# Seven modulation groups moved from the attentions into the first feed forward, and the softmax divisors turned in one matmul

## What is computed

```python
s_lat = silu(c);  s_ctx = silu(c_ctx)
for i in range(2):
    ml = split(s_lat @ w_ada[i] + b_ada[i], 6)     # w_ada[i] is 1024 x 6144
    mc = split(s_ctx @ w_ada[i] + b_ada[i], 6)     # the context needs none of layer 1 but shift and scale
    u = rms_norm(h, g_pre_mix[i]) * (1 + ml[1]) + ml[0]
    h = h + ml[2] * rms_norm(mixer(u), g_post_mix[i])
    f = mlp(rms_norm(h, g_pre_ff[i]) * (1 + ml[4]) + ml[3])     # square of relu, width 4096
    h = h + ml[5] * rms_norm(f, g_post_ff[i])
```

## Time and profile before

| | us |
|---|---|
| median of three runs (lowest, highest) | 1934.95 (1932.95, 1937.16) |
| the profiled execution | 1936.78 |
| its span | 1934.9 |

### The profile page before, as it was taken

The page is one execution under the profiler, slowest core; times in us unless marked ns, Lnnn a source line. Parts: engine busy times, 40 slices in busy tenths (PEclk is TensorE's granted clock), DMA queues, the critical chain, the costliest instruction groups (busy, mean ns, idle before and its releaser), DMA issues. The chain is left out here.

```text
span 1934.9 us, 37112 instructions
## 1 busy us (share of the span) xinstructions
PE 1869.8 (97%) x15824; PEld 1559.3 (81%) x15824; DVE 1105.8 (57%) x1835; ACT 861.6 (45%) x1559; POOL 211.9 (11%) x249
## 2 busy tenths in 40 slices
PE   7999999999999999999999999999999999899998
PEld 5768998776899788756898888888887798579986
DVE  6566774566667554476557665444444565546643
ACT  5465653446656542465322335322222254655532
POOL 2101221110122100103122211000000011000000
PEclk9999999999999999999999999999999999899999
DMA  7777665467766541353000042333332234024653
GB/s 267 250 256 224 189 183 175 166 227 263 223 166 195 175 142 55 115 174 110 26 4 4 4 151 65 104 119 98 100 107 88 66 99 139 25 88 133 194 180 124
DMA packets 219354, 264.68 MB, mean 137 GB/s; under 512 B 14214, under 2 KB 153782, under 8 KB 214711
## 3 DMA queue, kind: packets, MB, share of 16 engines
q1 hardware_dynamic: 218603, 261.49, 42.4%
q10 hardware_dynamic: 588, 0.82, 0.1%
HBM read 261.20 MB, written 1.09 MB: 136 GB/s over the span
## 5 line engine op out<-in xcount | busy, mean ns | idle before, releaser
L404 PE MATMUL acc<-rounded,rounded 128*128 128x512 f32 (+1 forms) x2552 | 875.1, 343 | 9.6 <-DVE rounded L684 4.1
L405 PE MATMUL acc<-rounded,rounded 128*128 128x512 f32 (+1 forms) x2552 | 867.0, 340 | 0.0
L406 PE MATMUL acc<-rounded,rounded 128*128 128x512 f32 (+1 forms) x2552 | 866.8, 340 | 0.0
L388 DVE TENSOR_TENSOR rounded<-arena,rounded 128x2048 fp32r<-128x2048 f32 (+1 forms) x194 | 434.3, 2241 | 285.9 <-ACT rounded L377 285.8
L404 PEld LDWEIGHTS acc<-rounded,rounded 128*128 128x128 f32 x2552 | 480.6, 188 | 80.1 <-issue 14.7
L405 PEld LDWEIGHTS acc<-rounded,rounded 128*128 128x128 f32 x2552 | 480.7, 188 | 60.0 <-issue 1.9
L406 PEld LDWEIGHTS acc<-rounded,rounded 128*128 128x128 f32 x2552 | 480.5, 188 | 60.0
L377 ACT ACTIVATE rounded<-arena 128x2048 fp32r<-128x2048 f32 (+1 forms) x194 | 362.9, 1873 | 341.6 <-PE acc L406 296.4
L1624 DVE SCALAR_TENSOR_TENSOR arena<-acc,pcol,arena 128x254 f32<-128x254 f32 (+1 forms) x176 | 76.8, 478 | 52.3 <-ACT arena L1605 50.8
L2200 PE MATMUL sc<-arena 64*64 64x64 f32 x2560 | 94.7, 221 | 8.8 <-DVE arena L2350 7.7
L2764 ACT ACTIVATE arena<-acc 128x512 f32<-128x512 f32 (+1 forms) x64 | 31.4, 490 | 159.6 <-PE acc L406 159.6
(11 more groups left out here) (265 smaller groups left out, 1691.6 us busy)
## 6 DMA issues: line engine op xcount, KB each, us to landing
arena<-in_w_ff SPq DMA_DIRECT2D x64, 1024.0 KB, 5.4
arena<-in_w_ada SPq DMA_DIRECT2D x48, 1024.0 KB, 5.1
arena<-in_w_up SPq DMA_DIRECT2D x88, 512.0 KB, 5.1
arena<-in_w_in SPq DMA_DIRECT2D x24, 1024.0 KB, 5.3
arena<-in_w_down SPq DMA_DIRECT2D x20, 1024.0 KB, 5.0
arena<-in_w_out SPq DMA_DIRECT2D x16, 1024.0 KB, 5.1
arena<-in_w_in_even SPq DMA_DIRECT2D x9, 1024.0 KB, 5.3
arena<-in_w_in_odd SPq DMA_DIRECT2D x8, 1024.0 KB, 5.2
```

The costliest lines, as they stand in the source:

```text
L388: dve.tensor_tensor(r32(w), w, r32(high_slot(c)[:, 0:size(c)]), ALU.subtract).then_inc(split_made, 1)
L404: pe.matmul(ps, ah, bh, start=first, stop=False)
L405: pe.matmul(ps, ah, bl, start=False, stop=False)
L406: return pe.matmul(ps, al, bh, start=False, stop=last)
```

## The change

Four things are changed.

- **Late groups.** Groups 16 to 22 leave the attentions. Their 14 chunks are put into the load order of ff0, one ahead of each of ff1(1) to ff1(7) and of ff2(0) to ff2(6). VectorE multiplies the four 128x512 rows of such a chunk by a column of `silu_c` each and adds them up in `late_sum` (`late_dve`, four chained instructions), before it splits the chunk two places behind. TensorE sums over the partitions against a column of ones (`late_pe`, four matmuls of 2 columns, in the second block of ff2(e)); VectorE adds the bias (`late_add`). Group 23 stays, in units 0 and 1 of attBl.
- **Divisors.** POOL copies the two reciprocals of a unit into a 128x128 tile (`widen`), and TensorE turns it with one transpose in place of the two matmuls of L903. This holds for all 48 featured units. `prep_pool`'s products are placed between these copies.
- **Order on VectorE.** The decays go ahead of the rotation of the queries, behind the eight cumulative sums; the key preparations go with units 0 to 7.
- **Gates.** The gates of layer 0 are transposed in scan step 1 and stored alone; those of layer 1 get a transpose, a copy and their stores in and behind the projection of layer 1.

```diff
+        def plan_late():
+            n = len(late_chunk)
+            view = I["w_ada_2"][1].rearrange("(k p) n -> p k n", p=P)
+            c, k0 = 512 * (4 + n // 2), 4 * (n % 2)
+            late_chunk.append(len(chunks))
+            whole.add(len(chunks))
+            chunks.append(view[:, k0:k0 + 4, c:c + 512])
+            release.append((late_read, n + 1))
...
             while splits["low"] < len(split_chunks) and split_chunks[splits["low"]] <= g:
                 n = splits["low"]
                 c = split_chunks[n]
+                late_dve(dve, c)
                 dve.wait_ge(high_made, n + 1)
...
-        plan_ada(range(16, 20), lambda n: sc_at["attBl"] + 3 * n)
-        plan_ada(range(20, 24), lambda n: sc_at["attBc"] + 3 * n)
+        plan_ada([23], lambda n: sc_at["attBl"])
...
         def plan_ff1(e):
+            if e:
+                plan_late()
...
         def plan_ff2(e):
+            if e < EIGHTHS - 1:
+                plan_late()
...
-                pe.wait_ge(att_comb, self.base + u + 1)
-                for m in range(2):
-                    ins = pe.matmul(ps[m * HD:(m + 1) * HD, P:2 * P], self.recip[:, 2 * u + m:2 * u + m + 1].broadcast_to([P, HD]), ident,
-                                    start=True, stop=True, tile_position=(0, m * HD))
+                i = self.featured.index(u)
+                pe.wait_ge(att_wide, self.spread_units + i + 1)
+                ins = pe.transpose(ps[:, P:2 * P], self.wide[:, i % 2, :], ident)
...
+            def widen(self, pool, before=None):
+                for i, u in enumerate(self.featured):
+                    if before and u in before:
+                        before[u]()
+                    pool.wait_ge(att_comb, self.base + u + 1)
+                    if i >= 2:
+                        pool.wait_ge(att_spread, self.spread_units + i - 1)
+                    pool.tensor_copy(self.wide[:, i % 2, :].rearrange("p (m e) -> p m e", m=2),
+                                     self.recip[:, 2 * u:2 * u + 2].unsqueeze(2).broadcast_to([P, 2, HD])).then_inc(att_wide, 1)
...
+        def late_dve(dve, c):
+            while late_done[0] < len(late_chunk) and late_chunk[late_done[0]] + 2 <= c:
+                n = late_done[0]
+                late_done[0] += 1
+                if n and n % 2 == 0:
+                    late_add(dve, n // 2 - 1)
+                g = late_chunk[n]
+                wait_landed(dve, g)
+                if n % 2:
+                    dve.wait_ge(late_read, n)
+                w = shaped(raw_slot(g), g)
+                for k in range(4):
+                    s = silu_c[:, 4 * (n % 2) + k, 0:1]
+                    if n % 2 == 0 and k == 0:
+                        ins = dve.tensor_scalar(late_sum, w[:, k, :], s, None, ALU.mult)
+                    else:
+                        ins = dve.scalar_tensor_tensor(late_sum, w[:, k, :], s, late_sum, ALU.mult, ALU.add)
+                    if k < 3:
+                        link(dve, ins)
+                ins.then_inc(late_read, 1)
+
+        def late_pe(pe, b):
+            pe.wait_ge(late_read, 2 * b + 2)
+            ps = claim(pe, "tr", tr_at[("late", b)])
+            for n in range(4):
+                ins = pe.matmul(ps[:, 2 * n:2 * n + 2], late_sum[:, n * P:(n + 1) * P], ones[:, 0:2], start=True, stop=True)
+            ins.then_inc(tr_full, 1)
...
@@ projB_dve, behind the eight sums
+            for d in range(2):
+                decays_dve(dve, d)
...
@@ under_latent_dve
-                if u < 2:
-                    decays_dve(dve, u)
-                else:
-                    kd_dve(dve, *divmod(u - 2, 4))
+                if u < 8:
+                    kd_dve(dve, *divmod(u, 4))
...
@@ step_dve, s == 0
-                ada_gains(dve, att_bc.ada_tr[-1], 1)
+                wait_drained(dve, "tr", tr_at[("group_turn", 3)])
+                pre_gain(dve, 1, 0).then_inc(mod_ready, 1)
...
@@ ff0_tensor, between the chunks of ff2(e)
+                    if block == 1 and n == 0:
+                        late_pe(pe, key[1])
```

More of the change, by code:

```diff
@@ L327, in plan_ada @@
                 release.extend([(chunk_read, partial[0]), (sc_full, fill_of(n) + 1)])
+        late_read = sem("late_read")
+        late_chunk = []
+        def plan_late():
[7 more added lines that the diff above has]
+            if n % 2:
+                stage(("late", n // 2), tr=1)
         def is_up(g):
@@ L816, in __init__ @@
                 self.ada = list(ada) if ada is not None else []
-                self.sc = [sc_at[key] + u + (u // 2 + 1 if self.ada else 0) for u in range(n)]
+                self.sc = [sc_at[key] + u + min(u // 2 + 1, len(self.ada)) for u in range(n)]
                 self.base = att_units[0]
@@ L1240, in first_and_second_block, with late_add @@
         mod_ready = sem("mod_ready")
-        mod_gates = mod_gate.rearrange("p l w k s -> p (l w k s)")
+        gates_of = [mod_gate[:, l].rearrange("p w k s -> p (w k s)") for l in range(DEPTH)]
+        late_done = [0]
+        def late_dve(dve, c):
[6 more added lines that the diff above has]
+                wait_landed(dve, g)
+                if n % 2:
+                    dve.wait_ge(late_read, n)
[15 more added lines that the diff above has]
+            ins.then_inc(tr_full, 1)
+        def late_add(dve, b):
+            f = tr_at[("late", b)]
+            ps = filled(dve, "tr", f)
+            dve.tensor_tensor(mod[:, 1, 16 + 4 * b:20 + 4 * b, :], ps[:, 0:8].rearrange("p (a b) -> p a b", a=4),
+                              col("b_ada_2", 6 * KT + 16 + 4 * b, 4).unsqueeze(2).broadcast_to([P, 4, 2]), ALU.add)\
+               .then_inc(drain("tr", f), 1)
         def ada_pe(pe, att, i, n):
@@ L1329, in group_dve, with pre_gain, post_gate, ada_gains @@
                .then_inc(drain("tr", f), 1)
[L1331 to L1342, removed]
+        def pre_gain(dve, l, w):
+            scale = mod[:, l, (3 * w + 1) * KT:(3 * w + 2) * KT, :]
+            pre = col(("g_pre_mix_2", "g_pre_ff_2")[w], KT * l, KT).unsqueeze(2).broadcast_to([P, KT, 2])
+            return dve.scalar_tensor_tensor(mod_gain[:, l, w], scale, 1.0, pre, ALU.add, ALU.mult)
+        def post_gate(dve, l, w):
+            gate = mod[:, l, (3 * w + 2) * KT:(3 * w + 3) * KT, :]
+            post = col(("g_post_mix_2", "g_post_ff_2")[w], KT * l, KT).unsqueeze(2).broadcast_to([P, KT, 2])
+            return dve.tensor_tensor(mod_gate[:, l, w], gate, post, ALU.mult)
+        def ada_gains(dve):
+            wait_drained(dve, "tr", tr_at[("group_turn", 2)])
+            for w in range(2):
+                pre_gain(dve, 0, w)
+                post_gate(dve, 0, w).then_inc(mod_ready, 1)
+        def late_gains(dve):
+            wait_drained(dve, "tr", tr_at[("late", EIGHTHS - 2)])
+            wait_drained(dve, "tr", att_bl.ada_tr[0])
+            pre_gain(dve, 1, 1)
+            for w in range(2):
+                post_gate(dve, 1, w).then_inc(mod_ready, 1)
         QK = {0: 0, 1: 1, 3: 2, 4: 3}
@@ L1732, in first_and_second_block @@
         at_ff0_end = r4.at
+        late_sum = Region(at_ff0_end + 9 * SEQ).take(512)
         r4 = Region(at1)
@@ L2077, in prep_pool, with key_rates, place @@
             pool.wait_ge(prep_done, 8)
-            for d in range(2):
-                for j in range(4):
-                    wait_drained(pool, "tr", att.more[3 if d else j])
-                    pool.tensor_tensor(kka[d][:, j, :], kk[:, j, :], rates[d][:, j, :], ALU.mult).then_inc(kka_done, 1)
+            def key_rates(*pairs):
+                def place():
+                    for d, j in pairs:
+                        wait_drained(pool, "tr", att.more[3 if d else j])
+                        pool.tensor_tensor(kka[d][:, j, :], kk[:, j, :], rates[d][:, j, :], ALU.mult).then_inc(kka_done, 1)
+                return place
+            att.widen(pool, {1: key_rates((0, 0)), 2: key_rates((0, 1)), 3: key_rates((0, 2)), 4: key_rates((0, 3), (1, 0)),
+                             5: key_rates((1, 1), (1, 2)), 6: key_rates((1, 3))})
             for d in range(2):
@@ L2877, in first_and_second_block @@
         spread2 = Region(at_y2).take(2, P)
+        wide2 = Region(at_y2 + 2 * P).take(2, P)
         yT2 = uT1
@@ L3142, in _ @@
                     wait_drained(sp, "tr", tr_at["gates"])
-                    for post in posts.values():
-                        post.gate_out(sp)
+                    mix0.gate_out(sp)
+                    ff0.gate_out(sp)
                 if g == chunk_at["out2_0"] + 1:
```

68 lines of the change are left out of this document (42 added, 26 removed).

## The result

After takes 1927.75 us against 1937.05 us of before: ratio 0.995, 95% interval 0.9937 to 0.9964, 9.3 us faster by the medians. The forecast was -17.9 us; a gain of 9 to 13 us came. The sign and the order of the stages were right, the size was not. Of the 10.7 us between the forecast 1917.1 and 1927.75, 2.1 come from the start: before's median was 1934.95 us over the three runs that the forecast rests on and is 1937.05 over six.

What follows compares the result with a forecast made beforehand. TensorE, busy 97% of the span, was taken as the bound, with VectorE taking over in attBl. Terms -7.7 - 10.3 - 0.3 - 3.0 - 3.0 + 6.2 + 0.2 = -17.9 us gave 1917.1 us on the median, range 1911 to 1927.

Steps and rivals of the forecast that it cites:

- Divisors: All 48 attention units: one transpose for L903's four instructions saves 0.19 us a unit, 9.1 us in all.
- The rival: Divisors bring nothing, through a switch between tile shapes or the wait for POOL: 9.1 us missing, 1926; chance 0.06.
- attBl: Attention stage attBl: with the modulation gone VectorE binds at 3.63 us a step; 34.6 us, 7.7 less than 42.3.
- attBc and entry: Stage attBc with the entry into the scan: no engine binds alone; 29.6 us against 39.9, 10.3 less.
- ff0: Stage ff0: seven column sums on TensorE add 6.2 us, late gates' transpose and small pieces 0.2; VectorE's chunks stay hidden.
- The tightest place: VectorE in ff0: the split at 1508.68, behind a late chunk, ends at 1514 with 3 us to spare.
- The clock: Rival: attBl and attBc idle more, three more clock dips plus POOL in VectorE's way give +8 us, 1925; chance 0.20.
- What was costed at nothing: POOL's copy and the decays ahead of the queries' rotation, ff0's loads, and the gates' stores and load: no time added.
- 826.4: Warning sign: the prediction is wrong if the rotation of the queries (L1802) starts later than 826.4.
- 3 us less of gain in attBl: If POOL's copies hit attBl's key preparations, with two SBUF inputs, in each unit, the gain is some 3 us less.
- TensorE as the only bound: Rival: TensorE stays the bound throughout and its removed work counts whole, -25.5 us, 1909.5; chance 0.07.
- slower by a stall of ff0: Rival: late chunks delay split, drains and slot reload in ff0; 3.0 us showing 14 times gives +24, 1959; chance 0.07.

Runs made afterwards that it cites:

- e1: The kernel before with only the new divisors (POOL's copy and one transpose a unit), no modulation moved: 1931.43 us against 1936.21, ratio 0.9978.
- e2: The kernel after with the old divisors (two matmuls, no POOL copy), the modulation still moved: 1931.08 us, ratio 0.9972 to before.
- e12: The kernel after unchanged, measured again; its profile is the third of after: 1924.92 us against 1937.82 of before, ratio 0.9938.
- e4: The kernel after with the late chunk of ff2's sixth round moved behind the first four drains: 1931.27 us, ratio 0.997 to before.
- e8: The kernel after with attBc's minimum against the sink (L969) made by two one-column scalar-operand instructions: 1925.01 us, ratio 0.9945 to before.

## Why the prediction was wrong, step by step

- **Divisors (-9.1 us): the step that failed.** It priced a transpose inside a run of eight, 0.13 us, against the 0.32 us of four matmuls that include the wait at the change of tile width, and called the difference saved. The runs show 0.06 us a unit, 2.9 us in all; as whole kernels 3.4 and 3.5 at an equal mean clock (e1, e2). Of the 9.1 us the sum holds 7.5, since attBl is priced by VectorE; for the 40 units outside attBl 2.4 came. These 5 us are the largest part of what is missing. The rival named the switch, but took the whole 9.1 us as lost and gave it 0.06: of two forms with a different tile shape the rows held one only. Its 1926 lies near the measured time, but by luck: only some 5 us are missing here, the rest in other steps.
- **attBl (-7.7): right in kind, 1.3 to 1.4 us short.** VectorE became the bound, in steps of 3.61 us as worked out (3.63), but every second step is 4.11, because the divisors' transpose comes late there. From the first maxima to the end of the last it is 27.3 us in e12, for 26.8 priced with the waits; the larger miss is the end, 7.3 us from the last maxima to attBc for 5.5 priced, where ScalarE's copies come late. 35.97 us came for 34.6, in which 1 us stood for the unknown.
- **attBc and entry (-10.3): -11.4**, of which 1.7 belong to the dip of the earlier trace rows in before; so some -9.7, 0.6 short. (The 1.7 is an estimate: half of the 3.4 us at half the clock.)
- **ff0 (+6.2 and 0.2): +7.0 to 7.7.** The column sums cost 0.89 us each, as priced. VectorE's chunks cost 2.8 to 3.0 us each, as priced, and were hidden thirteen times in fourteen. The tightest place was sought at the split; it was in the sixth round, whose drains for the near bias the prediction didn't look at: 1.3 us.
- **The clock** was a rival at 0.20, priced with more dips in attBl and attBc: 1925. It is real and smaller: a new dip at the entry of the scan in each of the three profiles of after (some 1.4 us), one at the start of attBl in one of them, against which stands the one that left attD. In the mean it is 0.0005 to 0.0008 of the clock, about 1 us.
- **What was costed at nothing** and was: POOL's copy (0.29 us, and TensorE waited for it 0.3 us in all), the decays (the stage ahead of attBl is 4.09 us in before and in e12), gates and loads. The rotation of the queries starts at 826.67 in after, past the 826.4 that was to be a warning, but the whole timeline stands 0.3 us later there: the turn of rows 7 starts at 572.69 in place of 572.40. The prediction also named 3 us less of gain in attBl, should POOL's copies and the key preparations, with their two SBUF inputs, meet in each unit. That didn't come: the sixteen instructions of the key preparations last 0.67 to 0.69 and 0.75 us in after, 0.68 and 0.75 in before; one copy of POOL ran beside one of them, and it was the copy that took longer, 0.67 us in place of 0.29. POOL's product held L969 longer than before (six times in eight over 0.6 us; four in before), at most 0.8 us.
- **TensorE as the only bound, and slower by a stall of ff0**, did not come; the latter happened once in fourteen places, and e4 shows how close it is: moving one chunk cost 5.8 us.

Summed by stages, the third profile of after against before, with the dip of attD taken as 1.7 us: the two att1 are 2.4 us short, attC and attD 1.3, attBl 1.4, attBc 0.6, ff0 0.6 to 1.3. That is 6.3 to 7.0, and 17.9 less that is near 11; the runs have 10 to 12 at an equal clock and 9 to 13 as measured.

## What to carry to other kernels

Price a replaced instruction by the time from its neighbour before to its neighbour after, in the order in which the new form will stand: a wait for a change of tile shape does not go away with the instruction that showed it. Work that is put on an engine that idles half the time is hidden only if each of its places is looked at, and with it everyone who waits for it, not just the tightest place of one kind. Removing work from the engine that binds can lower its granted clock as well, here by little; a filler must not be longer than the idle time that it fills.

## What the runs showed of the hardware

- From tiles 64 columns wide to tiles of 128, TensorE waits 0.1 us (e1: the values up to the first tile of 128 take 0.37 in place of 0.27 us for four matmuls; in attBl of after 1.02 in place of 0.92 for sixteen).
- A VectorE instruction of two columns with two SBUF tensors waited up to 1.03 us for the end of a POOL instruction; a tensor_scalar of one column on the same tile did not wait (0.20 to 0.22 us, all sixteen of e8).
- A column sum by TensorE of a 128x512 tile costs 0.89 us in a dense stream, although each of its matmuls moves two columns: it has eight weight loads of 0.19 us (56 for the seven groups), overlapped in part.
- A mean clock lower by 0.001 goes with 1.5 to 1.7 us more, over the 40 executions of before and the 17 of after.
